# Four of the eight modulation units of the second layer's value slabs go from TensorE to VectorE

## What is computed

```python
def adaln(cond, w, b):
    m = jax.nn.silu(cond) @ w + b
    m = m.reshape(cond.shape[0], 6, 1, D_MODEL)
    return [m[:, j] for j in range(6)]

def modulate(x, g, shift, scale):
    return rmsnorm(x, g) * (1 + scale) + shift
...
        sh1p, sc1p, g1p, sh2p, sc2p, g2p = adaln(c_ctx[None], w_ada[l], b_ada[l])
        sh1s, sc1s, g1s, sh2s, sc2s, g2s = adaln(c, w_ada[l], b_ada[l])
...
        xp = xp + g1p * rmsnorm(yp, norm_g[l, 1])
        xs = xs + g1s * rmsnorm(ys, norm_g[l, 1])
```

## Time and profile before

| | |
|---|---|
| time, 3 runs | 2535.63 us median, 2533.28 to 2539.55 |
| profiled execution | 2532.77 us, span of the records 2530.8 us |
| TensorE (PE) | 2466.9 us busy, 97% of the span |
| VectorE (DVE) | 1540.9 us, 61% |
| ScalarE (ACT) | 1044.6 us, 41% |
| GpSimd (POOL) | 196.8 us, 8% |
| DMA | 645.02 MB, 255 GB/s over the span |
| TensorE's granted clock | 0.992 of full speed, mean |

### The profile page before, as it was taken

One profiled execution on the slowest core, in us unless ns is written; L12 is line 12 of the kernel. 1 busy time (PEld: TensorE's weight loads), 2 busy tenths in 40 slices (PEclk: granted clock), 3 DMA queues, 4 the chain that ended last, 5 costly groups with the idle time before them and its releaser, 6 DMA issues.

```text
span 2530.8 us, 36183 instructions
## 1 busy us (share of the span) xinstructions
PE 2466.9 (97%) x14130; PEld 2007.5 (79%) x14130; DVE 1540.9 (61%) x1652; ACT 1044.6 (41%) x1134; POOL 196.8 (8%) x334
## 2 busy tenths in 40 slices
PE   6899999989999999999999999999999999999998
PEld 3578888778788788888877777797788888888887
DVE  2244445476777777776564464565787778655565
ACT  3233334363333333334453365584634343343343
POOL 0020000000010010000000032200011001000000
PEclk8999999999999999999999999999999999999999
DMA  9999888968889889888768954457577667656554
GB/s 360 358 289 296 290 283 285 349 235 291 302 272 294 291 274 287 303 291 268 266 209 273 314 179 164 152 192 269 184 236 266 217 228 265 220 178 207 190 194 174
DMA packets 467024, 645.02 MB, mean 255 GB/s; under 512 B 14184, under 2 KB 333480, under 8 KB 464872
## 3 DMA queue, kind: packets, MB, share of 16 engines
q1 hardware_dynamic: 445056, 568.61, 67.2%
q0 software_dynamic: 19504, 73.65, 8.1%
q10 hardware_dynamic: 2360, 1.32, 0.2%
HBM read 630.19 MB, written 13.34 MB: 254 GB/s over the span
## 4 chain that ended last, share of the span: by engine, by line
PE 71%; DMA 11%; DVE 8%; ACT 5%; issue 3%; ACTq 1%; SPq 0%; DVEq 0%
PE PS L1324 17%; PE PS L1405 11%; PE PS L1406 11%; PE PS L1407 11%; PE PS L1327 9%; DMA RAW<-in_w_mlp 6%; DVE WLO L1920 4%; ACT WHI L1647 3%; PE PS L1353 3%; DMA RAW<-in_w_o_na 2%; DMA RAW<-in_w_o_gla 2%; DMA SCR<-in_w_ada 1%; PE PS L1543 1%; PE PS L1544 1%; PE PS L1545 1%
## 5 line engine op out<-in xcount | busy, mean ns | idle before, releaser
L1920 DVE TENSOR_TENSOR WLO<-RAW,WHI 128x2048 fp32r<-128x2048 f32 x382 | 870.2, 2292 | 669.9 <-ACT WHI L1647 669.0
L1647 ACT ACTIVATE WHI<-RAW 128x2048 fp32r<-128x2048 f32 x382 | 726.4, 1913 | 708.2 <-DMA RAW<-in_w_mlp 481.9
L1324 PE MATMUL PS<-HM,WHI 128*128 128x512 f32 x2560 | 649.7, 396 | 1.6 <-issue 1.6
L1324 PEld LDWEIGHTS PS<-HM,WHI 128*128 128x128 f32 x2560 | 460.3, 189 | 100.6 <-issue 16.3
L1405 PE MATMUL PS<-WHI,HID 128*128 128x512 f32 x1152 | 452.4, 393 | 12.0 <-DVE WLO L1920 12.0
L1406 PE MATMUL PS<-WLO,HID 128*128 128x512 f32 x1152 | 449.1, 390 | 0.0
L1407 PE MATMUL PS<-WHI,HID 128*128 128x512 f32 x1152 | 448.9, 390 | 0.0
L1327 PEld LDWEIGHTS PS<-HM,WLO 128*128 128x128 f32 x2560 | 349.2, 190 | 26.2 <-DVE WLO L1920 0.6
L1327 PE MATMUL PS<-HM,WLO 128*128 128x256 f32 x2560 | 356.9, 282 | 0.2 <-DVE WLO L1920 0.2
L1405 PEld LDWEIGHTS PS<-WHI,HID 128*128 128x128 f32 x1152 | 216.5, 188 | 64.6 <-issue 16.3
L1407 PEld LDWEIGHTS PS<-WHI,HID 128*128 128x128 f32 x1152 | 216.7, 188 | 45.6
(11 more groups left out here) (250 smaller groups left out, 1848.3 us busy)
## 6 DMA issues: line engine op xcount, KB each, us to landing
RAW<-in_w_mlp SPq DMA_DIRECT2D x256, 1024.0 KB, 5.9
ADW<-in_w_ada SPq DMA_DIRECT2D x138, 1024.0 KB, 9.0
RAW<-in_w_qkv_na SPq DMA_DIRECT2D x46, 1024.0 KB, 7.0
X<-in_w_ada POOLq DMA_DIRECT2D x128, 256.0 KB, 4.0
RAW<-in_w_qkvg_gla SPq DMA_DIRECT2D x32, 1024.0 KB, 7.2
SCR<-in_w_ada SPq DMA_DIRECT2D x16, 1024.0 KB, 11.5
RAW<-in_w_o_na SPq DMA_DIRECT2D x16, 1024.0 KB, 7.4
RAW<-in_w_qkvg_gla SPq DMA_DIRECT2D x32, 512.0 KB, 4.6
```

The lines of the kernel that those rows point to most:

```text
L1324: return mm(bank[:, 0:2 * T2], hi[:, k, P * b:P * b + P], act[:, kc, 0:2 * T2], start=first, stop=False)
L1647: actv(WHI[:, 2 * s + u, 0:n], RAW[:, u, 0:n], ACT.Copy).then_inc(hi_done, 1)
L1920: tt(WLO[:, 2 * s + u, 0:n], RAW[:, u, 0:n], WHI[:, 2 * s + u, 0:n].bitcast(f32), ALU.subtract).then_inc(lo_done, 1)
```

## The change

Four of the eight units of the value slabs become a quad (number QV = 3) on VectorE, in X's space.

- PLAN_V becomes one unit a slab, four in all: TensorE makes one after piece 0 of each value slab.
- POOL parks X a second time, in `gla_pool`, behind the loads and memsets that it did there before, and then loads the 16 tiles of the quad (`value_quad`). X comes back (`return_x(QV + 1)`) in the key slabs, behind the first rotation.
- VectorE waits for the second half of the park to land ahead of its first `split_lo` of the value stage, and works on 15 tiles inside the value slabs (V_TILES) and on the last behind the `split_lo` of pieces 2 and 3 of the first key slab.
- TensorE sums the partitions (`quad_rows`) after piece 1 of the first key slab, into PSUM bank 7 and with a table PICKS_V of its own; ScalarE copies and stores the rows after its next pair of `split_hi`. The first product that uses bank 7 after that (`final_state`) waits for the copy.
- The numbers of units, of parks and of returns that other waits count up to move on by one quad.

```diff
-        A_WO1 = A_QKV1 + 2 * NB
+        A_WO1 = A_QKV1 + NB
...
-        PLAN_WO0, PLAN_WO, PLAN_V = ((0, 1), (2, 3), (4, 5), ()), ((0,), (1,), (), ()), ((0, 1), (2, 3), (4, 5), (6, 7))
+        PLAN_WO0, PLAN_WO, PLAN_V = ((0, 1), (2, 3), (4, 5), ()), ((0,), (1,), (), ()), ((0,), (1,), (2,), (3,))
...
+        V_TILES = ((0, 3), (2, 2), (2, 2), (2, 2))
...
@@ gla_tensor: final_state, between
+                else:
+                    pe.wait_ge(quad_row, QV + 2)
...
+                    if r == R_QK and p == 3:
+                        quad_rows(QV, 2, PICKS_V, QUADS_VB)
@@ gla_scalar
                 split_hi(M_QKV1 + r + 1, (r + 1) % 2, UNIT, range(2), r + 2 - R_QK if r + 1 < R_G else 0)
+                if r == R_QK + 1:
+                    quad_store(QV, QUAD_UNITS[QV], QROW_V, QUADS_VB)
@@ gla_vector
                 split_lo(M_QKV1 + r + 1, (r + 1) % 2)
+                if r == R_QK:
+                    value_tile(KC - 1)
@@ gla_pool
             end.then_inc(sem("low_rank_ones"), 1)
+            pool.wait_ge(sem("low_rank_ones"), 1)
+            value_quad()
+            pool.wait_ge(pick_ready, 2 * 2)
             pool.wait_ge(ada_done, A_WO1 + 1)
...
             rotate(0)
+            return_x(QV + 1)
@@ block.vector
+            def value_slab(n):
+                m = M_QKV1 + 2 * n
+                split_lo(m + 1, 1)
+                value_tiles(n, 0)
+                split_lo(m + 2, 0)
+                value_tiles(n, 1)
+                for b in range(2):
+                    evacuate_out(m, n, b, False, VG, WIDE, b + 7)
...
+            dve.wait_ge(x_parked[1], 16 * 2)
             for n in range(YN):
                 if n == 1:
                     gla_low_rank_vector(dve)
-                out_slab(M_QKV1, n, False, None, False, VG, WIDE)
-            gla_vector(dve, link, split_lo, evacuate)
+                value_slab(n)
+            gla_vector(dve, link, split_lo, evacuate, value_tile)
@@ block.gpsimd
+            def value_quad():
+                park_x(2, 4, PICKS_V)
+                for k in range(KC):
+                    quad_load(QV, k)
```

More of the change, by code:

```diff
@@ L191, in build_program @@
         BETWEEN = {0: A_MLP0 - 1, 1: A_QKV1 - 1, 2: A_MLP1 - 1}
-        QUAD_UNITS = [A_MLP0 + GU * g + PU for g in range(QUADS0)] + [A_MLP1 + SKIP, A_END - QU]
-        assert A_MLP1 + SKIP + 2 * QU - 1 == A_END
+        QUAD_UNITS = [A_MLP0 + GU * g + PU for g in range(QUADS0)] + [A_WO1 + SKIP, A_MLP1 + SKIP_V, A_END - QU]
+        assert A_MLP1 + SKIP_V + 2 * QU - 1 == A_END
         raw_in = [sem("raw_in0"), sem("raw_in1")]
@@ L269, in build_program @@
         ROWSUM_T = CB[:, 1024:1024 + P]
-        QROW = CB[:, 1152:1152 + UC]
-        PICK = [CB[:, 1408 + 32 * b:1440 + 32 * b] for b in range(2)]
+        QROW, QROW_V = CB[:, 1152:1152 + UC], CB[:, 1792:1792 + UC]
+        PICKS, PICKS_V = CB[:, 1408:1472], SCR[:, 2 * S4 + 2048:2 * S4 + 2112]
+        QUADS_VB = psum[7]
         XF = X[:, :, :].rearrange("p b n -> p (b n)")
@@ L281, in build_program @@
         UP_TILES = KC - sum(OUT_TILES)
+        V_TILES = ((0, 3), (2, 2), (2, 2), (2, 2))
+        assert sum(map(sum, V_TILES)) == KC - 1
         QUAD_SLOT = [k % 2 for k in range(KC)]
@@ L661, in gla_low_rank_vector, with gla_tensor @@
             end.then_inc(sem("low_rank_ready"), 1)
-        def gla_tensor(pe, unit, wide_unit, body):
+        def gla_tensor(pe, unit, wide_unit, body, quad_rows):
             mm, turn = nc.tensor.matmul, nc.tensor.transpose
@@ L821, in gla_tensor, with gla_scalar @@
             return turn_out
-        def gla_scalar(act, split_hi):
+        def gla_scalar(act, split_hi, quad_store):
             actv = nc.scalar.activation
@@ L1054, in gla_vector, with gla_pool @@
             out_lo(3)
-        def gla_pool(pool):
+        def gla_pool(pool, value_quad, return_x):
             tt = nc.gpsimd.tensor_tensor
@@ L1243, in _ @@
             for n in range(YN):
-                load_out(M_QKV1, n, wq1, 0, range(4), plan_ada(PLAN_V[n], A_QKV1, 1), 2 * KEY)
+                load_out(M_QKV1, n, wq1, 0, range(4), plan_ada(PLAN_V[n], A_QKV1, SKIP), 2 * KEY)
             for h in range(GLA_H):
@@ L1613, in _ @@
                 out_slab(M_QKV1, n, FULL(HM), filled(3), value_ada, None, WIDE)
-            turn_out = gla_tensor(pe, unit, out_unit, tokens_out(HM))
+            turn_out = gla_tensor(pe, unit, out_unit, tokens_out(HM), quad_rows)
             def output_ada(n, x):
@@ L1659, in store_row, with quad_store @@
                                   MROW[b:P:32, :].rearrange("p (h n) -> p h n", h=2)).then_inc(row_out, 16)
-            def quad_store(q, unit):
+            def quad_store(q, unit, row=QROW, bank=ROWS_TB):
                 act.wait_ge(quad_summed, q + 2)
                 act.wait_ge(quad_out, q * (16 * QU) + 16)
-                actv(QROW, ROWS_TB[:, 0:UC], ACT.Copy).then_inc(quad_row, 1)
+                actv(row, bank[:, 0:UC], ACT.Copy).then_inc(quad_row, 1)
                 act.wait_ge(quad_row, q + 2)
@@ L1891, in _ @@
                 out_slab(M_QKV1, n, tuple((A_QKV1 + at, A_QKV1 + SKIP + at) for at in PLAN_V[n]), None, False, 1 if n == YN - 1 else 0)
-            gla_scalar(act, split_hi)
+            gla_scalar(act, split_hi, quad_store)
             for n in range(YN):
-                out_slab(M_WO1, n, tuple((A_WO1 + at, A_WO1 + SKIP + at) for at in PLAN_WO[n]), 2)
+                out_slab(M_WO1, n, tuple((A_WO1 + at, A_WO1 + SKIP_V + at) for at in PLAN_WO[n]), 2)
             finish_stage(M_WO1, 2, 1, 3)
-            mlp(1, M_MLP1, None, QUADS0, QU - 1)
+            mlp(1, M_MLP1, None, QV + 1, QU - 1)
         @block.vector
@@ L1996, in quad_out_tile, with value_tile, value_tiles, out_slab @@
                     quad_tile(q, k, QUAD_SLOT[k], QUAD_SLOT[:k].count(QUAD_SLOT[k]))
-            def out_slab(m0, n, add, f=None, last=False, dst=Y, banks=YB, quad=None):
+            def value_tile(k):
+                quad_tile(QV, k, QUAD_SLOT[k], QUAD_SLOT[:k].count(QUAD_SLOT[k]))
+            def value_tiles(n, part):
+                first = sum(map(sum, V_TILES[:n])) + sum(V_TILES[n][:part])
+                for k in range(first, first + V_TILES[n][part]):
+                    value_tile(k)
+            def value_slab(n):
[6 more added lines that the diff above has]
+                    evacuate_out(m, n, b, False, VG, WIDE, b + 7)
+            def out_slab(m0, n, add, f=None, last=False, quad=None):
                 m = m0 + 2 * n
@@ L2024, in out_slab @@
                 for b in range(2):
-                    evacuate_out(m, n, b, add, dst, banks, b + 7)
+                    evacuate_out(m, n, b, add, Y, YB, b + 7)
             def evacuate_out(m, n, b, add, dst, banks, ends):
@@ L2361, in _ @@
             load_gain(2)
-            park_x(2, 3, 6)
-            for q in range(QUADS0, QUADS0 + QUADS1):
+            park_x(3, 6, PICKS)
+            for q in range(QV + 1, QV + 1 + QUADS1):
                 for k in range(KC):
                     quad_load(q, k)
-            return_x(QUADS0 + QUADS1)
+            return_x(QV + 1 + QUADS1)
             load_gain(3)
```

57 lines of the change are left out of this document (30 added, 27 removed).

## The result

The changed kernel takes 2543.93 us (median of 15 runs, 2536.49 to 2548.39), the kernel before 2534.70 beside it (15 runs): +9.2 us, a ratio of 1.0036 with a 95% interval of 1.0028 to 1.0044. I had forecast no measurable difference, with an upper end of 2543.0. The profiled execution took 2542.28 us, 2540.4 us of it the span of the records.

A forecast was written before the change was run, and what follows sets the result against it. TensorE and the DMA were taken as nearly full in the value slabs. -8.3 + 1.1 + 1.7 + 3.8 + 1.6 = -0.1 us on the median 2535.6 gave 2535.5, no measurable difference, range 2530.0 to 2543.0.

The forecast's parts named there:

- The units and the sums: TensorE: four modulation units of 2.07 us go, -8.3 us; the sums of one quad come, +1.1 us.
- The wait for the park: Value slab 0: TensorE waits ahead of piece 2 for VectorE's split, held by the park; +1.7 us, bounds 0 and 5.0.
- The wait for the last tile: First key slab: TensorE waits between pieces 1 and 2 for tile 15; +3.8 us, bounds 0 and 7.4.
- c: Value slabs: time of one turn of the loop of load, split_hi, split_lo, load; taken as 12.4 us.
- 8c - 95.4: Formula for TensorE's wait for the last tile, eight loop turns after the stage's first pair of splits; +3.8 us.
- at the speed of the DMA: Value slabs: the loop runs at the DMA's speed, not that of freed slots; ScalarE waited 80.9 us for loads.
- nearly full: Value slabs: TensorE and the DMA are nearly full, the DMA at a share of 0.94 with 325 GB/s.
- The bytes of a slab stay: Value slabs: 4 MB of pieces, 2 MB of units, 2 MB of tiles in place of the other two units.
- The clock: TensorE: one fall of the granted clock charged for an idle time of 3.8 us; +1.6 us, bounds 0 and 3.2.
- Hidden work: VectorE's some 39 us of tiles, X's return and ScalarE's stores cost 0; VectorE waits some 2 us in slab 0.
- rival (c): Scans: TensorE's gain is taken back by X's return or ScalarE's stores; 2540.9 us at most, chance 0.05.
- Rival (b): Slabs 1 to 3: late tiles hold VectorE's splits, each turn grows, price eightfold; 13.5 us turns give 2544.3; chance 0.25.

The follow-up runs named there:

- all_small: The changed kernel with tile work, tile loads and the park cut to a few columns (results wrong); 2527.72 us, -6.5 against the kernel before.
- half_units: The changed kernel with the first half of each unit's load (slab 0's excepted) issued half a slab earlier, bytes unchanged; 2533.86 us, -0.4 against the kernel before.
- spread2: The changed kernel with VectorE's park wait moved to the first tile, sums later, 13 tiles in the value slabs, three later; 2529.24 us.
- spread3: late_both with 14 tiles in the value slabs, two behind the first key slab's splits, tile 2 no longer ahead of slab 0's copies; 2531.41 us.
- late_both: The changed kernel with VectorE's park wait at the first tile, sums after piece 3 of the first key slab, ScalarE's stores later; 2533.96 us.

## Why the prediction was wrong

- **The units and the sums (-8.3 and +1.1): right.** all_small shows 6.5 of 7.2 us in the medians, and 6.9 from the first matmul of slab 0 to the first gates (127.3 and 120.4 us).
- **The wait for the park (+1.7): right in place, and in size partly by luck, 1.28 us.** (Its own terms, 1352.1 less 1350.5, are 1.6.) POOL issued the park 7.9 us after X was ready (forecast 7.7), and it landed 8.3 us after that (forecast 7.3): 1.3 us later in all. TensorE came to the piece 1.8 us later than forecast as well, because of a low clock (below), and that covered it. The estimate by the Trainium skill, page "DMA: Bandwidth & Descriptors", section "Anatomy of one DMA", was 6.8 us for the two halves; the trace does not agree, it took 1.5 longer, beside the last loads ahead of it. What I missed is that much of the late start carries through the loop: moving the wait gave 4.0 us, not 1.3.
- **The wait for the last tile (+3.8): here it failed**, in "So I take c between its nearest rows, 11.88 and 12.85: 12.4". The turn measured 13.35. My formula, 8c - 95.4, gives 11.4 us for that, and TensorE's waits after the park are 7.46 + 4.25 = 11.7 us, so the formula held (three of its other terms moved by 1 to 3 us and cancelled, which is luck) and its c did not. Both rows were the wrong ones: in those turns the units came at TensorE's beat, by SP's 67.0 us of waiting for it, and in every half slab, so they showed neither how fast the loop could go nor how it would go with its loads in other places. The reading behind it, that the loop runs "at the speed of the DMA", came from ScalarE's waits, which only say that loads come last, not what let them start. And the eight turns of the kernel before, from its first pair at 1344.42, are 13.76 us each: slab 0 turns slowly, and my sum went over eight turns with a number from the last four. That the DMA is "nearly full" was read from one window, too; the one from 1370 to 1383 has a share of 0.38.
- **"The bytes of a slab stay": true, and not enough.** 32.7 MB moved from 1345 to 1455 before and 32.3 after. But a slab's bytes now came as 5 MB in one turn and 3 in the next, and half_units shows that moving half of each unit, with the bytes unchanged, was worth 10 us.
- **The clock (+1.6): right** where I charged it, 1.9 us behind the wait of 7.5. A second low stretch stands in the first 4 us of the stage, where the kernel before had one in the 4 us ahead of it (0.66):

```profile
1334.66:1338.66 4.00, 4.00 (x11) 3.15 (x12) 3.80 (x10) 1.22 (x2) 2.71 (x3) 0.57 1.05 387
```

0.43 of 4.00 us are 1.7 us. Nothing shows that the change put it there: five of the thirteen changed kernels have it in their profile, spread2 among them, and eight have not.
- **Hidden work.** The tiles were not quite free: tile 2 of slab 0 held VectorE for 4.11 us where I had said 2. The return of X and ScalarE's stores were hidden: from the first gates to the last head's turns both kernels take 146 us, so rival (c) didn't happen.
- **The sum with measured terms**: -8.3 + 1.1 + 1.3 + 11.7 + 1.9 = +7.7 of 9.2 us. With the second low stretch it is +9.4, where the two traces differ by 10.8 from the first matmul of slab 0 to the first gates (127.3 and 138.1 us); the rest I can't assign. **Rival (b)** had the sign, the place and the price (c = 13.5 gave 2544.3), but its mechanism is only a small part: VectorE waited 5.2 us in all for tiles, 4.1 of them once, and spread3, without that wait, was 2.8 us below late_both. I gave it 0.25, and 0.11 for a loss that can be measured.

## What to carry to other kernels

Before taking a loop's turn from a trace, ask what its first step waits for: a queue that waits for the consumer shows the consumer's beat, not the loop's own speed. Count bytes by turn, not by slab: loads that come in every other turn only should be dealt out over the turns. And place a wait for a chain's end, and a wait that gates the chain's start, where their consumers first need them; here these two places, with ScalarE's stores moved behind the second, were worth 9 us of a change that had 7 to give.

## What was not expected of the hardware

- A piece of 1 MB took 6 us to land in one turn and 13.4 in the next, with the DMA at 371 to 373 GB/s in the latter: the 2 MB ahead of it in SP's queue and the tiles beside it set it, not its own size.
- Taking 2 MB a slab from SP's queue or from POOL's gave the same time within the scatter: 4.4 and 4.5 us below the kernel before, with intervals some 5 us wide.
- Two DMAs of 1 MB from X took 8.3 us together, beside the last loads ahead of them, where a lone one had taken 4.1.
